# Wide products for the high halves of the weights in the gate, up and down stages of eight networks

## The reference

```python
def swiglu(h, w_gate, w_up, w_down):          # w_gate, w_up: 1024 x 2816, w_down: 2816 x 1024
    return (silu(h @ w_gate) * (h @ w_up)) @ w_down
```

## Time and profile before

| | |
|---|---|
| median of 3 timed executions | 3004.48 us |
| profiled execution, its time | 3005.31 us |
| its span | 3003.3 us |
| TensorE busy | 2856.4 us (95%), 26460 products |
| VectorE busy | 1981.6 us (66%) |
| ScalarE busy | 1465.0 us (49%) |
| bytes moved | 511.10 MB, mean 170 GB/s |
| mean granted TensorE clock | 0.974 |

### The profile page before, as it was taken

The page is one execution under the profiler, slowest core; times in us unless marked ns, Lnnn a source line. Parts: engine busy times, 40 slices in busy tenths (PEclk is TensorE's granted clock), DMA queues, the critical chain, the costliest instruction groups (busy, mean ns, idle before and its releaser), DMA issues.

```text
span 3003.3 us, 60757 instructions
## 1 busy us (share of the span) xinstructions
PE 2856.4 (95%) x26460; PEld 2727.2 (91%) x26460; DVE 1981.6 (66%) x2927; ACT 1465.0 (49%) x2199; POOL 13.0 (0%) x23
## 2 busy tenths in 40 slices
PE   7999999999999999899899899998999999998999
PEld 7999777889999997777899899987999999998899
DVE  6667556667677677566676666566767667776654
ACT  5445534445454455344354444465445445766543
POOL 0000000000000000000000000000000000000000
PEclk9999989999999999899999999898999999999999
DMA  6674301246656753111456566532665764342353
GB/s 232 239 267 171 112 33 45 83 146 234 237 213 250 263 189 114 57 44 44 155 209 230 193 231 234 186 126 94 230 250 203 250 246 155 129 153 99 141 183 141
DMA packets 72793, 511.10 MB, mean 170 GB/s; under 512 B 8464, under 2 KB 9104, under 8 KB 11728
## 3 DMA queue, kind: packets, MB, share of 16 engines
q1 hardware_dynamic: 72528, 507.21, 46.8%
HBM read 506.13 MB, written 1.05 MB: 169 GB/s over the span
## 4 chain that ended last, share of the span: by engine, by line
PE 85%; DVE 8%; ACT 5%; issue 2%; DMA 0%; SPq 0%; DVEq 0%; ACTq 0%
PE linear_banks L1917 21%; PE linear_banks L1918 20%; PE linear_banks L1919 20%; PE linear_banks L2418 3%; PE linear_banks L2419 3%; PE linear_banks L2420 3%; PE solve_banks L2281 1%; DVE split_halves L1277 1%; PE solve_banks L2005 1%; PE linear_banks L2247 1%; PE solve_banks L2290 1%; DVE squares L1358 1%; PE solve_banks L2377 1%; PE solve_banks L2467 1%; DVE rstd L1313 1%
## 5 line engine op out<-in xcount | busy, mean ns | idle before, releaser
L1277 DVE TENSOR_TENSOR split_halves<-raw_units,split_halves 128x1024 fp32r<-128x1024 f32 x806 | 979.6, 1222 | 516.8 <-ACT split_halves L889 514.9
L889 ACT ACTIVATE split_halves<-raw_units 128x1024 fp32r<-128x1024 f32 x806 | 845.7, 1055 | 626.8 <-PE linear_banks L1919 489.3
L1917 PE MATMUL linear_banks<-h_split,split_halves 128*128 128x256 f32 x3456 | 998.2, 289 | 25.1 <-DVE split_halves L1277 13.8
L1918 PE MATMUL linear_banks<-h_split,split_halves 128*128 128x256 f32 x3456 | 982.2, 284 | 0.0
L1919 PE MATMUL linear_banks<-h_split,split_halves 128*128 128x256 f32 x3456 | 981.8, 284 | 0.0
L1917 PEld LDWEIGHTS linear_banks<-h_split,split_halves 128*128 128x128 f32 x3456 | 666.7, 193 | 40.5 <-issue 21.5
L1918 PEld LDWEIGHTS linear_banks<-h_split,split_halves 128*128 128x128 f32 x3456 | 666.9, 193 | 2.0 <-issue 1.9
L1919 PEld LDWEIGHTS linear_banks<-h_split,split_halves 128*128 128x128 f32 x3456 | 666.9, 193 | 0.0
L1917 PE MATMUL linear_banks<-hidden_split,split_halves 128*128 128x256 f32 x1408 | 397.5, 282 | 0.0
L1919 PE MATMUL linear_banks<-hidden_split,split_halves 128*128 128x256 f32 x1408 | 394.8, 280 | 0.0
L1918 PE MATMUL linear_banks<-hidden_split,split_halves 128*128 128x256 f32 x1408 | 394.8, 280 | 0.0
(11 more groups left out here) (319 smaller groups left out, 3820.5 us busy)
## 6 DMA issues: line engine op xcount, KB each, us to landing
raw_units<-in_stream SPq DMA_DIRECT2D x403, 1024.0 KB, 4.8
raw_units<-in_mod_w SPq DMA_DIRECT2D x72, 1024.0 KB, 6.7
x<-in_x SPq DMA_DIRECT2D x4, 256.0 KB, 4.6
w2a<-in_w2a SPq DMA_DIRECT2D x2, 512.0 KB, 6.1
w_rows<-in_w SPq DMA_DIRECT2D x2, 512.0 KB, 8.0
bs_rows<-in_bs SPq DMA_DIRECT2D x2, 512.0 KB, 8.7
spatial_t<-in_ws_t SPq DMA_DIRECT2D x2, 512.0 KB, 11.0
out<-x SPq DMA_DIRECT2D x4, 256.0 KB, 4.2
```

What stands on the lines that cost most here:

```text
L889: nc.scalar.activation(split[:, n % SPLIT_SLOTS, 0, :], raw[:, item % RAW_SLOTS, (n % 2) * HALF * P:(n % 2 + 1) * HALF * P], ACT.Copy).the ...
L1277: V.tensor_tensor(split[:, n % SPLIT_SLOTS, 1, :], raw[:, item % RAW_SLOTS, (n % 2) * HALF * P:(n % 2 + 1) * HALF * P], split[:, n % SPLIT ...
L1917: M(o, w_hi, a_hi, start=start, stop=False, skip_group_check=skip)
L1918: M(o, w_hi, a_lo, start=False, stop=False, skip_group_check=skip)
```

## The change

- **Products.** In the late gate-and-up units (`unit_tiles`) and in all of the down stage, the high weight tile meets both halves of the activations in one product of 512 columns into a whole bank; the low weight tile then meets the high half in a product of 256 columns into the bank's first half. High by high and low by high gather in columns 0:256, high by low in 256:512, and the two have to be added afterwards. The early units keep three products of 256.
- **Banks.** A unit now takes a pair of banks (gate, up). Three pairs go round, two of `sv` and one of `lin`, and which comes first depends on whether i is even. The down sums alternate between two pairs of `sv`. The waits for free banks are written out (`unit_free`).
- **Engines.** ScalarE copies the second halves of both banks to `units` (128x512); VectorE adds the first halves to it and so frees the banks; the silu and the product read `units`. A down sum is added to `x` in two passes.
- **Modulation.** The dots move from units 1..18 to 4..21 and stand between the add and the product; their loads come three units later in SP's queue.
- **Head.** In the norm's step 3 VectorE makes the normed tile before the split; in step 4 ScalarE splits one half more before the last h tile (networks only), and VectorE does `first_unit(i, 0)` before it waits for that tile. Then the split of half 6 (`keep_ahead(base + 3)`), and then `first_unit(i, 1)`.

```diff
@@ mod_done and make_plan
-    return (j - 4) // 3 if j >= 4 and (j - 4) % 3 == 0 and (j - 4) // 3 < MOD_FFN else None
+    return (j - 5) // 3 if j >= 5 and (j - 5) % 3 == 0 and (j - 5) // 3 < MOD_FFN else None
...
-        at = [3 * m + 4 for m in range(MOD_FFN)]
+        at = [3 * m + 7 for m in range(MOD_FFN)]
@@ build_program
+    def unit_banks(i, j):
+
+        return (lin[:, 0:2, :] if i % 2 == 0 else sv[:, 0:2, :], sv[:, 2:4, :],
+                sv[:, 0:2, :] if i % 2 == 0 else lin[:, 0:2, :])[j % 3]
+
+    def down_banks(d):
+
+        return sv[:, 2 - 2 * (d % 2):4 - 2 * (d % 2), :]
@@ ScalarE, split_h and ffn
-                    if n in ROUGH and s in (2, 3):
+                    if n in ROUGH and (s in (2, 3) or s == 4 and n in FFN_OF):
                         keep_ahead(first_half_of(n) + s - 1)
...
-                    keep_ahead(base + 2 * j + 1)
+                    early = is_early(i, j)
+                    keep_ahead(base + (3 + j if early and j < 2 else 2 * j + 1))
                     n = FT * i + j
                     if n >= 3:
                         gated(act, *gu_key(n - 3)[1:])
...
+                    if not early:
+                        wait_filled(act, ("gu", i, j))
+                        nc.scalar.activation(units[:, n % 3, :, :], unit_banks(i, j)[:, :, T:2 * T], ACT.Copy)\
+                            .then_inc(rest_copied, 1)
                     if j:
                         hidden_high(i, j - 1)
+                    wait_emptied(act, ("gu", i, j))
+                    bias = unit_bias[:, n % 3, 0:1] if early and ffn_norm(i) >= 7 else 0.0
+                    nc.scalar.activation(silu[:, n % 3, :], units[:, n % 3, 0, :], ACT.Silu, bias=bias)\
+                        .then_inc(silu_ready, 1)
@@ VectorE, norm
                         elif s == 3:
+                            normed(n, m, 3)
                             keep_ahead(first_half_of(n) + 2)
-                            normed(n, m, 3)
                         elif s == 4:
                             normed(n, m, 4)
+                            if n in FFN_OF:
+                                first_unit(FFN_OF[n], 0)
@@ VectorE, ffn
+                    keep_ahead(base + (3 + j if early and j < 2 else 2 * j + 1))
                     if early and j == 0:
-                        first_unit(i, 0)
                         first_unit(i, 1)
-                        keep_ahead(base + 3)
-                    bank = wait_filled(dve, ("gu", i, j))
+                    elif early and j > 1:
+                        first_unit(i, j)
+                    elif not early:
+                        dve.wait_ge(rest_copied, LATE.index((i, j)) + 1)
+                        V.tensor_tensor(units[:, n % 3, :, :], unit_banks(i, j)[:, :, 0:T], units[:, n % 3, :, :],
+                                        ALU.add)\
+                            .then_inc(emptied["dve"], 1)
+                        wait_emptied(dve, ("gu", i, j))
+                    if i < MOD_NETWORKS and 4 <= j < 4 + 3 * MOD_FFN:
+                        for t in MOD_SPREAD[(j - 4) % 3]:
+                            mod_dot(MOD_AT["ffn", i, (j - 4) // 3], t)
+                    if j:
+                        hidden_rest(i, j - 1)
                     dve.wait_ge(silu_ready, n + 1)
...
-                        V.tensor_tensor(product[:, n % 3, :], silu[:, n % 3, :], bank[:, T:2 * T], ALU.mult)\
-                            .then_inc(emptied["dve"], 1)
-                    if i < MOD_NETWORKS and 0 < j <= 3 * MOD_FFN:
-                        for t in MOD_SPREAD[(j - 1) % 3]:
-                            mod_dot(MOD_AT["ffn", i, (j - 1) // 3], t)
-                    if j:
-                        hidden_rest(i, j - 1)
+                        V.tensor_tensor(product[:, n % 3, :], silu[:, n % 3, :], units[:, n % 3, 1, :], ALU.mult)\
+                            .then_inc(unit_gated, 1)
@@ VectorE, residual
+                if key[0] == "down":
+                    for part in range(2):
+                        both = down_banks(key[2])[:, :, part * T:(part + 1) * T]
+                        if factor is not None:
+                            ins = V.scalar_tensor_tensor(x[:, c:c + 2, :], both, factor, x[:, c:c + 2, :],
+                                                         ALU.mult, ALU.add)
+                        else:
+                            for i in range(2):
+                                ins = V.scalar_tensor_tensor(x[:, c + i, :], both[:, i, :],
+                                                             gate2[:, which, c + i:c + i + 1], x[:, c + i, :],
+                                                             ALU.mult, ALU.add)
+                        if part == 0:
+                            link(ins)
+                    ins.then_inc(emptied["dve"], 1)
@@ TensorE
+            def unit_free(i, j):
+
+                if j >= 3:
+                    wait_emptied(pe, ("gu", i, j - 3))
+                elif i and j:
+                    wait_emptied(pe, ("down", i - 1, j + 1) if i % 2 == 0 else (*X_FROM[ffn_norm(i)], j + 1))
+
+            def unit_tiles(w, i, j, ready):
+
+                unit_free(i, j)
+                banks = unit_banks(i, j)
+                order = [(e, k) for k in range(DT) for e in range(2)] if ready else \
+                    [(e, k) for e in range(2) for k in range(DT)]
+                halves = [half_ready(w), half_ready(w + 1)] if ready else []
+                for e, k in order:
+                    if ready and e == 0:
+                        ready(k)
+                    if not ready and k == 0:
+                        halves.append(half_ready(w + e))
+                    s, t = halves[e], slice(k * P, (k + 1) * P)
+                    M(pairs(banks[:, e, :]), s[:, 0, t], h[:, :, k, :], start=k == 0, stop=False)
+                    ins = M(banks[:, e, 0:T], s[:, 1, t], h[:, 0, k, :], start=False, stop=k == DT - 1)
+                    if k == DT - 1:
+                        ins.then_inc(halves_used if e == 0 else lin_filled, 1)
...
-                            ins = three(bank[:, e * T:(e + 1) * T], s[:, 0, t], s[:, 1, t], hidden[:, 0, k, :],
-                                        hidden[:, 1, k, :], k == 0, k == FT - 1)
+                            M(pairs(bank), s[:, 0, t], hidden[:, :, k, :], start=k == 0, stop=False)
+                            ins = M(bank[:, 0:T], s[:, 1, t], hidden[:, 0, k, :], start=False, stop=k == FT - 1)
```

70 lines of the change are left out of this document (31 added, 39 removed).

## The result

The changed kernel takes 2958.15 us (median of four, 2951.5 to 2960.2) against 3004.09 for the kernel before on the same chip: ratio 0.9844, 95% interval 0.9827 to 0.9861. So it is 46 us faster; I forecast 94, and the range ended just short of it, at 2958.0. The direction was right, the size was not. The profiled execution, the fastest of the four, has a span of 2949.8 us against 3003.3, and 4000 products fewer.

The account below looks back on a forecast made before the run. TensorE, busy 95% of the span, was taken as the bound: product count times cadence, plus idle places. 3003.3 - 90.4 (products) - 9 (heads) + 5 (residual, mixer heads) = 2908.9 us of span; forecast 2910, range 2885 to 2958.

Parts of the forecast that it names:

- The step that failed: Merged gate-and-up and down products: a 512-column product takes 215.5 ns, sized by the f32 sum-of-squares row.
- the prediction's own product sum: Tiles save 24.5 ns by 2592 in gate and up and 19.1 ns by 1408 in down, together 90.4 us.
- each load costs its share even under a long stream: Rival, merged products: the excess over columns stays on the 512-column product, 44 us saved, 2956 us; chance 0.12.
- the load sets the cadence: TensorE products: 16 and 256 columns both start 0.21 us apart at half clock, so the load alone can set the cadence.
- the cadence goes with columns: Rival, TensorE products: same columns, so no gain in products, 3000 us, no change; chance 0.04.
- Down: Down stage products: a tile goes from 352 to 333 ns, saving 26.9 us over 1408 tiles.
- the second residual pass: Adding down sums: plus 0.8 us behind network 3, 1.1 each behind 4, 6 and 7; plus 5 with mixer heads.
- Heads: Gate-and-up heads of rough networks: reordered splits and scalings leave some 3 of 12 us idle, minus 9 us.
- The mixer heads: Heads of the two mixers: plus 0.5 us each, counted within the plus 5 us.
- copies and adds at nothing: Late units: ScalarE's copy and VectorE's add stay hidden under TensorE, VectorE at 90%; price zero.
- modulation at nothing: Modulation dots and loads moved from units 1..18 to 4..21: counts stay, transfers not saturated; price zero.
- VectorE rival: Late units: handovers eat part, 2920 to 2955 us, chance 0.07; or VectorE becomes the bound, about 3037, chance 0.04.

Follow-up runs that it names:

- e15_one_place: Changed kernel with tiles 1 to 6 of each gate-and-up sum, by unit, as changed or rereading one place in fp32r, bf16 or f32; 3393.2 us.
- e2_three_again: Changed kernel with three products of 256 columns per tile again, all else kept; 2993.1 us, ratio 0.9972.
- e14_loads: Changed kernel with gate-and-up tiles 1 to 6, by unit, as changed, pure bf16, or with 64-column loads for the 512-column product or both; 2936.3 us.
- e4_low_16: Changed kernel with 16 instead of 256 columns in the second product of late and down tiles; 3068.2 us, one stretch at half clock.
- e11_widths: Changed kernel with gate-and-up products narrowed by unit: first product 128 to 448 columns, second 64 to 224; 2889.1 us.
- e13_kinds: Changed kernel with the first gate-and-up product, by unit, as changed, bf16 constants, overwriting the bank, or twice 240 columns; 2938.9 us.
- e3_no_low: Changed kernel without the 256-column low-weight product of late and down tiles; 2827.9 us.
- e8_old_head: Changed kernel with the heads of the networks in their old order; 2973.5 us, ratio 0.9901.
- e12_old_modulation: Changed kernel with modulation dots back at units 1 to 18 and their loads at the old places; 2958.3 us, ratio 0.9834.
- e1_adjacent: Changed kernel with the two halves of each activation tile side by side, read as one run of 512 columns; 2952.9 us, ratio 0.9843.
- e5_low_load_64: Changed kernel with low weights loaded 64 columns wide instead of 128, except in a sum's last tile; 2948.5 us, ratio 0.9820.
- changed_again: The changed kernel itself, unchanged, timed and profiled a second time; 2959.2 us, ratio 0.9839.

## Why the prediction was wrong

*The step that failed* is "I take 215.5, 213.3 and 2: the f32 row is the nearest, equally long and with its own load". It was equally long and of another type. On fp32r operands a 512-column product costs 230 ns, 17 above its columns; e15_one_place shows bf16 and f32 at 2 to 3 above and fp32r at 17, with the same reading pattern. Put 230 and 117 into the prediction's own product sum: gate and up 360 - 347 = 13 ns by 2592 tiles, 34 us; down 352 - 347 = 5 ns by 1408, 7 us; 41 instead of 90.4. Timed, the merge gave 35 to 38 (e2_three_again). The 49 to 55 us missing there are more than the miss of 48, and the heads made up for the rest.

*The bound was there and I left it.* The prediction had 213 to 240 for this product from its rows and chose the low end. 230 lies inside it; the range came from the chances of named rivals, and no case stood between 222 and 228 ns for it.

*The rival "each load costs its share even under a long stream"* had a chance of 0.12, gave 2956 and hit the time; its arithmetic (an excess that stays on the long product) is what happened, with a tile of 348 against 347. Its reason is shown only in part: a load half as wide takes 7 ns off a tile (e14_loads), the other 15 stay. That the time came out to 2 us is partly luck: it had 44 us for the products, which timed 35 to 38, and too little for the heads. The Trainium skill (TensorE: Matmul & The Clock Gate, the section on the back-to-back gap) gives columns / 2.4 + 2.5 ns for the gap between products, and calls that the gap of isolated ones, which the prediction left out. The bf16 rows, with a load for each product, agree with it (216 and 109 measured against 215.8 and 109.2), the fp32r rows don't (230 and 117). For a stream of loads and products the same section has about 131 ns at 512 columns; no run here shows less than 216.

*That the load sets the cadence* was right as a reading of rows 5 and is now shown at full clock (e4_low_16, e11_widths: about 112 ns a load). It doesn't follow that what a 256-column product needs above its columns is all load, which is how I used it.

*What the excess goes by.* Summed over a gate-and-up tile, where the split between neighbours doesn't matter, three products stand 40 ns above their 768 columns (360), two stand 27 above (346.7 in the shorter pattern), and two with 736 columns in all again 27 (333, e13_kinds). So the rival that the cadence goes with columns falls: the same 768 columns cost less in two products than in three. The rows come out at 13 ns for each fp32r product, whatever its width between 256 and 512 columns, and a merge saves one of them; this is theory A. The long product alone stands 13 to 23 above in gate and up (e3_no_low), and the old down tile has 34 for three, so 13 is a summary of rows and not a law.

*Down* was sized worst: 26.9 us predicted, 7 to 10 by the traces, 1 to 2 as timed. Its old tile was already short (352 ns by the prediction's windows, 354 by the starts), and the second residual pass costs nearly what I said, 0.7 to 0.9 us behind three networks and 0.9 at the end (4.7 us from the last product to the end of the span against 3.8), 3.5 in sum against 5.

*Heads*: minus 9 predicted for gate and up, and the trace has minus 10 of 12.6 us (0.3 is left in networks 0 to 4 together, 0.6, 0.8 and 0.7 in 5 to 7), so this term was right. The mixer heads were not: each had a gap of 1.45 us, of which 0 and 0.3 are left, where I had added 0.5. Together the heads gave 12 to 13 us against the kernel before. The 15 to 17 of e8_old_head are measured against the old order under the changed products, which waits longer than before (16.4 us idle against 14.2). The sum that stands, each term with some us of doubt: 35 to 38 for the merge, 12 to 13 for the heads, 3.5 back at the tails, 46.

*What was right*: copies and adds at nothing (no product in mid-stage waits for VectorE), VectorE 85% busy instead of 90 (the unit is longer), banks free in time, modulation at nothing (e12_old_modulation), transfers far from full, at 0.65 of the DMA engines' time (0.71 predicted, for a shorter unit). ScalarE does wait for transfers more often than before (112 times and 135 us in all on `in_stream`, against 45 and 108), but no product in mid-stage waits behind it. Neither VectorE rival came.

No experiment gave a version clearly faster than the changed kernel: e1_adjacent (0.9843) is the same within its interval, and e5_low_load_64 (0.9820) leaves work out.

## What to carry to other kernels

Size a product by a row of the same type, not only of the same length; where there is none, keep both ends of the bound in the range. Merging two products that share a weight tile is worth what one product costs above its columns, here 13 ns of 360 in gate and up and 7 of 354 in down, and nothing at half clock; the load that goes was hidden already, at 256 columns over a load of 112 ns. Count back what the merge moves to other engines and to the tail of a sum. When a scheduling change is part of the gain, as at these heads, look at every place that runs the same code: the mixer heads gained 1.45 and 1.15 us, about as much each as those of gate and up.

## What the runs showed of the hardware

- At full clock, starts 512 / 256 columns apart: fp32r 230 / 117 ns, bf16 216 / 109, f32 858 / 431 in two passes of 429 / 215.5, each with a load of its own (e14_loads, e15_one_place).
- Summed over a gate-and-up tile, fp32r products stand 13 ns each above their columns: 360 ns for three of 256 columns (e2_three_again), 346.7 for 512 and 256, 333 for 480 and 256 (e13_kinds). In down, three stand 34 above in sum and two 27.
- The fp32r excess is absent at half clock: 512 and 16 columns take 640 ns (e4_low_16), 768 cycles of 1.2 GHz, and so do 512 and 256 (changed kernel) and three times 256 (kernel before).
- The same program keeps a stage at 346.7 or at 353.3 ns a tile from end to end, and which stages have which changes from one execution to the next (changed kernel, changed_again).
- Two loads of 128 columns have a floor of 223 ns at full clock under products of 128 and 64 columns (e11_widths). One load hides under each product, not two: 512 and 16 columns take 340 ns (e4_low_16).
- A load of 128 columns lasts 98 ns in bf16 and 187 to 190 in fp32r and f32, one of 64 columns in fp32r 134 (e14_loads, e15_one_place).
- bf16 and fp32r products in turn lost the bf16 product's gain: tile 348 ns mixed, 325 pure bf16, 347 pure fp32r (e13_kinds). A single change from bf16 to fp32r cost nothing (338 ns for the two, e14_loads).
- With every second product short (e4_low_16, one execution), the granted clock stayed at 0.50 for 287 us behind a wait of 4.03 us, though TensorE then had no gap, and a kernel with 31% fewer columns in these stages was 2% slower than the one before.
